# The order of large and small products in a column slot of a split-precision kernel

## The chip, the core and the metric

The kernel runs on one core of one Trainium2 chip. The metric is the device time of one execution in microseconds; the program's only output is a 256 x 1024 array of float32. Before the change the median of three timed runs is 1666.28 us (1665.99 to 1666.77).

## The reference

Two transformer blocks run on the same 256 tokens, of width 1024. The first has two layers: FFN, a mixer (attention beside a gated linear recurrence in the first layer, a gated short convolution in the second), FFN. The second has one: FFN, a mixer (a Fourier part beside a bidirectional state-space scan), FFN; another 256 tokens of context go through its first FFN and a part of its mixer. Between them these make seven passes through an FFN of this form, with norms and residuals around it:

```
def swiglu(h, w_gate, w_up, w_down):
    return (jax.nn.silu(h @ w_gate) * (h @ w_up)) @ w_down
```

The shapes are 256 x 1024 for `h`, 1024 x 2816 for `w_gate` and `w_up`, 2816 x 1024 for `w_down`. The short convolution's mixer begins with a product of `h` with a matrix of 1024 x 3072. All of this is float32.

## The kernel before, in words

Every float32 operand of a large product is split into two parts of lower precision, `hi` and `lo`, and a product is made of three: hi x hi, lo x hi, hi x lo. ACT writes the `hi` part of a weight tile (`w_hi`, line 1135), DVE the `lo` part (`w_lo`, line 1768), from tiles of 128 x 1024 that SP's queue brings in. Such a tile is a slot; the stream has 564, and eight lie in a ring that both parts share. TensorE (PE) does the products in the order in which the code issues them; no scheduler moves them.

An FFN runs in eleven steps of 256 of its 2816 columns, each with four slots for gate and up and two for the product with `w_down` (`down_slot`, line 539, 512-column products into the bank `dn`). In the first FFN all steps have the activations as the stationary operand (`wide_slot`, line 494). In the other six, steps 2 to 9 do it the other way round: a slot holds 128 columns of the weight for all eight k-tiles, and the weights are the stationary operand. These are the column slots (`column_slot`, lines 515 to 529), four in a row into the four banks `gu[0]`, `gu[1]`, `tp[0]`, `tp[1]`, so six FFNs with eight steps make 48 groups of four. Behind each group stand the two `down_slot`s of the step before. In front of it stand, as a rule, the two of the step before that; in eight groups a transposition lies between (lines 635 and 659). The short convolution's mixer, `sc`, has 24 more column slots (lines 871 and 874).

A column slot makes its three products with two instructions for a k-tile:

- the large one, 512 columns: `w_hi` stationary, and `hT[:, :, k, :]` moving, which is `hi` and `lo` of the activations side by side (lines 524 and 528), into the whole bank `o`
- the small one, 256 columns: `w_lo` stationary, `hi` of the activations moving (lines 525 and 527), added to the first half of the bank

The two halves of the bank are added later by another engine. Each product has a weight load ahead of it, of 128 x 128, which the profile shows as PEld. Before a slot's first product TensorE waits for the slot's `w_lo` (`lo_ready`), and the last one signals `slot_used`.

Of the kernel before, what the change touches and what calls it, by code (L numbers as in the profile page):

```python
# [23 lines left out]
KT = D // P  # L24
TOK = 256
# [112 lines left out]
def build(nc, weights, ada_w, x_in, ctx_in, pre_rows, post_rows, small, mod, out):  # L138
    with ExitStack() as stack:
        def sb(name, shape, dt=F32):  # L140
            return stack.enter_context(nc.sbuf_tensor(name, shape, dt))
# [5 lines left out]
        w_hi = sb("w_hi", [P, RING, SLOT], F32R)  # L147
        w_lo = sb("w_lo", [P, RING, SLOT], F32R)
        hT = sb("hT", [P, 2, KT, TOK], F32R)
        hT_hi, hT_lo = hT[:, 0, :, :], hT[:, 1, :, :]  # L150
# [301 lines left out]
        def _(pe):  # L452
# [62 lines left out]
            def column_slot(n, o, at_half=lambda: None):  # L515

                pe.wait_ge(lo_ready, n + 1)
                r = n % RING
                for k in range(KT):
                    if k == KT // 2:  # L520
                        at_half()
                    c = slice(k * P, (k + 1) * P)
                    if k == 0:
                        pe.matmul(o, w_hi[:, r, c], hT[:, :, k, :], start=True, stop=False)  # L524
                        pe.matmul(o[:, 0:TOK], w_lo[:, r, c], hT_hi[:, k, :], start=False, stop=False)  # L525
                    else:
                        pe.matmul(o[:, 0:TOK], w_lo[:, r, c], hT_hi[:, k, :], start=False, stop=False)  # L527
                        m = pe.matmul(o, w_hi[:, r, c], hT[:, :, k, :], start=False, stop=k == KT - 1)  # L528
                m.then_inc(slot_used, 1)

            def down_slot(n, acts, k, start=False, stop=False, used=True):
# [95 lines left out]
            def ffn(s, n0):  # L627
# [50 lines left out]
                for j in range(2, STEPS - 1):  # L678
                    n = n0 + 10 + 6 * (j - 2)
                    if s == 0:  # L680
                        if j > 2:
                            act_transposed(j - 1)
                        for si in range(4):
                            wide_slot(n + si, si, both)
                        down(n + 4, j - 1)
                        continue
                    for si in range(4):
                        if j > 2 and si % 2 == 0:
                            pe.wait_ge((gate_summed, up_summed)[si // 2], COLUMN_N[s, j - 1])
                        elif si == 2:  # L690
                            pe.wait_ge(actT_lo_ready, TURN_N[s, 1, None])
                        if si == 3 and (s, j - 1) in ADA_TURN:
                            pe.wait_ge(mod_biased, 1 + ADA_TURN[s, j - 1])
                        column_slot(n + si, column_bank(si))
                    down(n + 4, j - 1)
                    if (s, j) in ADA_TURN:
                        pe.wait_ge(up_summed, COLUMN_N[s, j])
                        mod_transposed(ADA_TURN[s, j])
# [159 lines left out]
            def sc(s, n0):  # L858
                for q in range(3 * KT):
                    if q == 1:  # L860
                        context_x_tokens(1)
                    if q == 4:
                        context_b_tokens()
                    if q == 7:
                        context_states()
                    if q == 8:
                        pe.wait_ge(state_ready, 2)
                    if SC_BEFORE[q] is not None:
                        pe.wait_ge(sc_summed, SC_BEFORE[q] + 1)
                    if q:  # L870
                        column_slot(n0 + q, sc_bank(q))
                    else:
                        pe.wait_ge(hT_lo_ready, 2 * TT * s + TT)
                        column_slot(n0, sc_bank(0), lambda: pe.wait_ge(hT_lo_ready, 2 * TT * (s + 1)))
                out_proj(s, n0 + 3 * KT, range(KT), [[MIX0["sc"] + 1 + k // 2] * TT for k in range(KT)], apart=(0, 1))
# [1838 lines left out]
```

## Time and profile before

| | before |
|---|---|
| median of three timed runs | 1666.28 us |
| span of the profiled execution | 1665.4 us |
| PE busy | 1655.6 us (99%), 8756 products |
| PEld (weight loads) busy | 1415.4 us (85%) |
| DVE busy | 1229.5 us (74%) |
| ACT busy | 927.8 us (56%) |
| PE's share of the chain that ended last | 94% |
| lines 527 and 528 in `gu` and `tp`, share of the chain | 10% for each bank pair at 528, 5% at 527 |

The profiled execution's time is its span, 1665.4 us; the median of the timed runs lies 0.9 us above it. Products are pipelined: one lasts longer (0.39 us for 512 columns) than the time from its start to the next start. So PE's busy time says only that it is never idle. How long a row of products takes is read from the starts in the time line.

### The profile page before, as it was taken

Reading aid. Unit: us, or ns where it says so; the run is one execution under the profiler, and the core shown is the slowest. Engines: PE = TensorE matmul, PEld = TensorE weight load, DVE = VectorE, ACT = ScalarE, POOL = GpSimd, SP = SyncE. Lnnn points to the kernel's source line nnn. Section 1 sums busy time; section 2 is a strip of 40 time slices with the busy share of each in tenths; the row PEclk is TensorE's granted clock in tenths of the full one; section 3 lists DMA queues with packets and bytes.
Section 4 is the critical chain, followed back from the end, with each engine's and each line's share of the span. In section 5 each row is a group of like instructions: output and inputs, shape, how many; then the busy total and the mean of one; then the engine's idle time right before and its main releaser. Section 6 shows DMA issues by size and latency. Waiting matters only on the chain.

```text
span 1665.4 us, 22804 instructions
## 1 busy us (share of the span) xinstructions
PE 1655.6 (99%) x8756; PEld 1415.4 (85%) x8756; DVE 1229.5 (74%) x1630; ACT 927.8 (56%) x1396; POOL 148.0 (9%) x210
## 2 busy tenths in 40 slices
PE   9999999999999999999999999999999999999998
PEld 7888888888888888888899888888888889988887
DVE  6888776788888777776688876655766668986564
ACT  6655577655555455545566455554645458655553
POOL 1100100000211001110010011000002012310000
PEclk9999999999999999999999999999999999999999
DMA  8977552787859876687655557554667545357551
GB/s 292 340 261 258 170 191 103 248 295 256 286 174 334 261 247 215 258 301 256 203 166 182 169 174 265 200 189 141 225 213 252 186 144 203 108 180 244 189 190 64
DMA packets 99356, 359.32 MB, mean 216 GB/s; under 512 B 11184, under 2 KB 11440, under 8 KB 99248
## 3 DMA queue, kind: packets, MB, share of 16 engines
q1 hardware_dynamic: 92736, 335.59, 59.0%
q0 software_dynamic: 6368, 22.21, 4.3%
q8 instruction: 69, 1.13, 0.3%
q14 instruction: 39, 0.32, 0.1%
q10 hardware_dynamic: 144, 0.07, 0.0%
HBM read 356.70 MB, written 1.12 MB: 215 GB/s over the span
## 4 chain that ended last, share of the span: by engine, by line
PE 94%; DVE 3%; DMA 2%; issue 1%; ACT 0%; SPq 0%; DVEq 0%; POOLq 0%; POOL 0%; ACTq 0%
PE dn L539 28%; PE gu L494 19%; PE gu L528 10%; PE tp L528 10%; PE gu L527 5%; PE tp L527 5%; PE dn L509 4%; DMA raw<-in_weights 2%; PE gu L524 1%; PE tp L524 1%; PE tp L457 1%; PE dn L528 1%; PE gu L525 1%; PE tp L525 1%; PE dn L494 1%; DVE w_lo L1768 1%
## 5 line engine op out<-in xcount | busy, mean ns | idle before, releaser
L1768 DVE TENSOR_TENSOR w_lo<-raw,w_hi 128x1024 fp32r<-128x1024 f32 x520 | 639.2, 1240 | 217.3 <-ACT w_hi L1135 212.4
L1135 ACT ACTIVATE w_hi<-raw 128x1024 fp32r<-128x1024 f32 x520 | 549.4, 1059 | 322.5 <-PE dn L539 147.7
L494 PE MATMUL gu<-w_hi,hT 128*128 128x512 f32 x1056 | 328.9, 393 | 1.6 <-DVE w_lo L1764 1.1
L528 PE MATMUL gu<-hT,w_hi 128*128 128x512 f32 x728 | 259.6, 396 | 0.0
L528 PE MATMUL tp<-hT,w_hi 128*128 128x512 f32 x728 | 259.5, 396 | 0.0
L539 PE MATMUL dn<-w_hi,actT_hi 128*128 128x512 f32 x608 | 238.8, 393 | 0.0
L539 PE MATMUL dn<-w_lo,actT_hi 128*128 128x512 f32 x608 | 236.9, 390 | 0.0
L539 PE MATMUL dn<-w_hi,actT_lo 128*128 128x512 f32 x608 | 236.7, 389 | 0.0
L494 PEld LDWEIGHTS gu<-w_hi,hT 128*128 128x128 f32 x1056 | 195.6, 188 | 42.6 <-DVE hT L1776 1.5
L494 PE MATMUL gu<-w_lo,hT 128*128 128x512 f32 x528 | 205.9, 390 | 0.0
L527 PE MATMUL gu<-hT,w_lo 128*128 128x256 f32 x728 | 203.1, 279 | 0.0
L527 PE MATMUL tp<-hT,w_lo 128*128 128x256 f32 x728 | 203.0, 279 | 0.0
L528 PEld LDWEIGHTS gu<-hT,w_hi 128*128 128x128 f32 x728 | 136.6, 188 | 28.2
L528 PEld LDWEIGHTS tp<-hT,w_hi 128*128 128x128 f32 x728 | 136.6, 188 | 28.2
L527 PEld LDWEIGHTS tp<-hT,w_lo 128*128 128x128 f32 x728 | 137.3, 189 | 4.8
L527 PEld LDWEIGHTS gu<-hT,w_lo 128*128 128x128 f32 x728 | 137.2, 189 | 4.5
L1912 DVE CUSTOM_DVE_ANT_0 arena<-arena 128x1024 f32<-128x1024 f32 x112 | 135.8, 1239 | 0.3
L539 PEld LDWEIGHTS dn<-w_lo,actT_hi 128*128 128x128 f32 x608 | 114.1, 188 | 24.2
L539 PEld LDWEIGHTS dn<-w_hi,actT_lo 128*128 128x128 f32 x608 | 114.2, 188 | 23.4
L539 PEld LDWEIGHTS dn<-w_hi,actT_hi 128*128 128x128 f32 x608 | 114.2, 188 | 21.2
L494 PEld LDWEIGHTS gu<-w_lo,hT 128*128 128x128 f32 x528 | 99.1, 188 | 21.0
L2467 POOL TENSOR_SCALAR ms<-ssq 128x1 f32<-128x1 f32 x42 | 16.8, 400 | 933.0 <-ACT junk L1166 919.3
(366 smaller groups left out, 2092.3 us busy)
## 6 DMA issues: line engine op xcount, KB each, us to landing
raw<-in_weights SPq DMA_DIRECT2D x563, 512.0 KB, 4.3
arena<-in_ada_w SPq DMA_DIRECT2D x72, 512.0 KB, 4.3
post_row<-in_post_rows POOLq DMA_DIRECT2D x10, 512.0 KB, 5.6
pre_row<-in_pre_rows POOLq DMA_DIRECT2D x10, 512.0 KB, 7.2
mod_row<-mod POOLq DMA_DIRECT2D x9, 512.0 KB, 10.0
shift_row<-mod POOLq DMA_DIRECT2D x5, 512.0 KB, 9.8
x<-in_x_in SPq DMA_DIRECT2D x4, 256.0 KB, 6.0
arena<-in_c_rows POOLq DMA_DIRECT2D x2, 512.0 KB, 9.3
```

What stands on the lines that cost most here:

```text
L457: m = pe.transpose(in_bank(s, t, half)[:, q * P:(q + 1) * P], rows[:, t, k * P:(k + 1) * P], ident[:])
L494: m = pe.matmul(bank, h[:, k, t * P:(t + 1) * P], w[:, r, kk * 512:(kk + 1) * 512], start=k == 0 and q == 0, stop=k == KT - 1 and q == 2)
L509: m = pe.matmul(o, w[:, r, k * P:(k + 1) * P], h[:, k, :], start=k == 0 and q == 0, stop=k == KT - 1 and q == 2)
L524: pe.matmul(o, w_hi[:, r, c], hT[:, :, k, :], start=True, stop=False)
L525: pe.matmul(o[:, 0:TOK], w_lo[:, r, c], hT_hi[:, k, :], start=False, stop=False)
L527: pe.matmul(o[:, 0:TOK], w_lo[:, r, c], hT_hi[:, k, :], start=False, stop=False)
L528: m = pe.matmul(o, w_hi[:, r, c], hT[:, :, k, :], start=False, stop=k == KT - 1)
L539: m = pe.matmul(dn[:, t, c], a[:, k, :], w[:, r, c], start=start and q == 0, stop=stop and q == 2)
L1135: act.activation(o, i, ACT.Copy, **kw).then_inc(done, 1)
L1768: dve.tensor_tensor(w_lo[:, r, :], raw[:, n % RAW, :], w_hi[:, r, :].bitcast(F32), ALU.subtract).then_inc(lo_ready, 1)
L1912: m = dve.tensor_tensor_reduce(ada_out[:, v, :], w, c_row[:, v, :], 1.0, 0.0, ALU.mult, ALU.add, mod_cols[:, i, v:v + 1])
L2467: pool.tensor_scalar(ms[:, c], ssq[:, c, 0], eps, None, ALU.add).then_inc(pool_step, 1)
```

## The change

In a column slot the first k-tile had its large product first and the other seven their small product first. Now every k-tile has the large product first and the small one behind it. The first large product opens the bank's sum as before; the last small product closes it and signals `slot_used`, where it was the last large one. The products, their operands and their number stay the same. In the short convolution's first slot the wait in the middle (`at_half`) stands ahead of a large product now, where it was a small one.

```
-                    if k == 0:
-                        pe.matmul(o, w_hi[:, r, c], hT[:, :, k, :], start=True, stop=False)
-                        pe.matmul(o[:, 0:TOK], w_lo[:, r, c], hT_hi[:, k, :], start=False, stop=False)
-                    else:
-                        pe.matmul(o[:, 0:TOK], w_lo[:, r, c], hT_hi[:, k, :], start=False, stop=False)
-                        m = pe.matmul(o, w_hi[:, r, c], hT[:, :, k, :], start=False, stop=k == KT - 1)
+                    pe.matmul(o, w_hi[:, r, c], hT[:, :, k, :], start=k == 0, stop=False)
+                    m = pe.matmul(o[:, 0:TOK], w_lo[:, r, c], hT_hi[:, k, :], start=False, stop=k == KT - 1)
```

PE at the start of a group behind a row of 512-column products (line 539, the second column group of the second FFN), before the change:

```order
L539 MATMUL dn<-w_lo,actT_hi 128x512
L524 MATMUL gu<-hT,w_hi 128x512
L525 MATMUL gu<-hT,w_lo 128x256
L527 MATMUL gu<-hT,w_lo 128x256
L528 MATMUL gu<-hT,w_hi 128x512
L527 MATMUL gu<-hT,w_lo 128x256
L528 MATMUL gu<-hT,w_hi 128x512
```

The same place now, where line 523 is the large product, line 524 the small one, and line 535 is what was 539:

```order
L535 MATMUL dn<-w_lo,actT_hi 128x512
L523 MATMUL gu<-hT,w_hi 128x512
L524 MATMUL gu<-hT,w_lo 128x256
L523 MATMUL gu<-hT,w_hi 128x512
L524 MATMUL gu<-hT,w_lo 128x256
L523 MATMUL gu<-hT,w_hi 128x512
L524 MATMUL gu<-hT,w_lo 128x256
```

The third product of the group was a small one and is a large one; the second small one moved one place back.

PE at the border between the first and the second slot of that group, before the change:

```order
L527 MATMUL gu<-hT,w_lo 128x256
L528 MATMUL gu<-hT,w_hi 128x512
L524 MATMUL gu<-hT,w_hi 128x512
L525 MATMUL gu<-hT,w_lo 128x256
L527 MATMUL gu<-hT,w_lo 128x256
L528 MATMUL gu<-hT,w_hi 128x512
```

The same border now:

```order
L523 MATMUL gu<-hT,w_hi 128x512
L524 MATMUL gu<-hT,w_lo 128x256
L523 MATMUL gu<-hT,w_hi 128x512
L524 MATMUL gu<-hT,w_lo 128x256
L523 MATMUL gu<-hT,w_hi 128x512
L524 MATMUL gu<-hT,w_lo 128x256
```

The two large products in a row at the border and the two small ones behind them are gone.

## Rows read from the trace of the kernel before

**Rows 1.** The page: PE's busy time, the granted clock, the chain by engine.

```profile
PE 1655.6 (99%) x8756; PEld 1415.4 (85%) x8756; DVE 1229.5 (74%) x1630; ACT 927.8 (56%) x1396; POOL 148.0 (9%) x210
...
PEclk9999999999999999999999999999999999999999
...
PE 94%; DVE 3%; DMA 2%; issue 1%; ACT 0%; SPq 0%; DVEq 0%; POOLq 0%; POOL 0%; ACTq 0%
```

**Rows 2.** PE's waits: line, engine waited for, us in total, times, longest.

```profile
PE dn L594 <- DVE actT_hi L2441: 1.5, 1, 1.5
```

**Rows 3.** Time line of PE, one group: start us, us, engine, line, operation.

```profile
340.73 0.39 PE L524 MATMUL gu<-hT,w_hi 128*128 128x512 f32 x1
340.95 0.28 PE L525 MATMUL gu<-hT,w_lo 128*128 128x256 f32 x1
341.07 0.28 PE L527 MATMUL gu<-hT,w_lo 128*128 128x256 f32 x1
341.19 0.40 PE L528 MATMUL gu<-hT,w_hi 128*128 128x512 f32 x1
...
343.19 0.28 PE L527 MATMUL gu<-hT,w_lo 128*128 128x256 f32 x1
343.31 0.40 PE L528 MATMUL gu<-hT,w_hi 128*128 128x512 f32 x1
343.54 0.40 PE L524 MATMUL gu<-hT,w_hi 128*128 128x512 f32 x1
...
344.00 0.40 PE L528 MATMUL gu<-hT,w_hi 128*128 128x512 f32 x1
...
346.08 0.40 PE L528 MATMUL gu<-hT,w_hi 128*128 128x512 f32 x1
346.32 0.39 PE L524 MATMUL tp<-hT,w_hi 128*128 128x512 f32 x1
...
349.13 0.40 PE L524 MATMUL tp<-hT,w_hi 128*128 128x512 f32 x1
...
351.91 0.39 PE L539 MATMUL dn<-w_hi,actT_hi 128*128 128x512 f32 x1
```

**Rows 4.** Line 524, whole program: counts, durations ns min/median/max, first and last start.

```profile
L524 PE MATMUL gu<-hT,w_hi x104: 389/397/501, 324.0 to 1623.4; 128*128 128x512 f32 x104
...
L524 PE MATMUL tp<-hT,w_hi x104: 393/397/527, 329.7 to 1629.0; 128*128 128x512 f32 x104
...
L524 PE MATMUL dn<-hT,w_hi x8: 389/395/398, 917.0 to 947.8; 128*128 128x512 f32 x8
```

**Rows 5.** Lines 528 and 527 from 341.2 to 343.3 us.

```profile
L528 PE MATMUL gu<-hT,w_hi x6: 395/398/403, 341.2 to 343.0; 128*128 128x512 f32 x6
...
L527 PE MATMUL gu<-hT,w_lo x7: 278/281/284, 341.1 to 343.2; 128*128 128x256 f32 x7
L527 PEld LDWEIGHTS gu<-hT,w_lo x6: 188/190/192, 341.2 to 343.0; 128*128 128x128 f32 x6
```

**Rows 6.** Lines 528 and 527 from 344.02 to 346.07 us.

```profile
L528 PE MATMUL gu<-hT,w_hi x6: 392/394/395, 344.0 to 345.7; 128*128 128x512 f32 x6
...
L527 PE MATMUL gu<-hT,w_lo x7: 274/274/280, 343.9 to 346.0; 128*128 128x256 f32 x7
L527 PEld LDWEIGHTS gu<-hT,w_lo x6: 187/188/188, 344.0 to 345.7; 128*128 128x128 f32 x6
```

**Rows 7.** Line 525 at 341.0 us.

```profile
L525 PE MATMUL gu<-hT,w_lo x1: 278/278/278, 341.0 to 341.0; 128*128 128x256 f32 x1
```

**Rows 8.** Line 525's weight load behind a transposition, at 324.1 us.

```profile
L525 PEld LDWEIGHTS gu<-hT,w_lo x1: 192/192/192, 324.1 to 324.1; 128*128 128x128 f32 x1
```

**Rows 9.** Time line of PE, first and last start of 16 convolution slots.

```profile
916.98 0.39 PE L524 MATMUL dn<-hT,w_hi 128*128 128x512 f32 x1
...
961.72 0.39 PE L539 MATMUL dn<-w_hi,actT_hi 128*128 128x512 f32 x1
```

**Rows 10.** The chain of waits from 860 to 915 us: start us, us, what.

```profile
869.65 7.68 DMA raw<-in_weights
```

## The prediction

> **What bounds the kernel now.** I read the page first, then TensorE's waits, the time line of one group of column slots, and last the durations inside single slots. The engine table has PE busy in 1655.6 of 1665.4 us, the clock row is at its top in every slice (2.4 GHz, the higher of its two levels), and the chain that ended last lies on PE for 94% [rows 1]. The waits agree: the longest total that PE spends on another engine is 1.5 us [rows 2]. So TensorE is the bound, what counts is the distance from the start of one product to the start of the next, and a nanosecond that the change adds there is a nanosecond of the whole, as long as no other engine is then late. None becomes late when TensorE gets slower.
>
> The reader is to look at starts, not at busy times. A large product (512 columns) starts 0.23 us before the next, a small one (256) about 0.12 us before it. Inside a column slot they already alternate. In the slot at 340.73, from the large product at 341.19 to the one at 343.31, there are six pairs in 2.12 us: 0.3533 us a pair. In the next slot, from 344.00 to 346.08, six like pairs take 2.08 us: 0.3467 [rows 3]. The instructions are the same, at the same clock, and nothing waits between them. So there are two paces, which I call loose and tight, and a slot keeps the one that it has to its end. The four slots take 2.81, 2.78, 2.81 and 2.78 us: the pace changes at every slot border [rows 3]. That border is where the alternation breaks: two large products in a row (343.31, 343.54), then two small ones. The change takes away just these breaks.
>
> **The change part by part.** It removes no product, adds none and moves no wait to another engine: 216 slots (104 + 104 + 8) [rows 4] of eight large and eight small products each. In a slot the order "large, small, small, large, small, large ..." becomes "large, small, large, small ...", also across the border to the next slot. What is moved is the order alone, so the sum has one big term: which pace an unbroken group runs at.
>
> By columns the swap is free: two large products in a row start 0.23 apart (343.31, 343.54) and two small ones 0.12 (340.95, 341.07), so two of each cost what two pairs cost [rows 3]. By paces it is not. Without a break nothing flips the pace, so all four slots of a group run at the one with which it begins. Groups of four (eight in each of six FFNs, 48 by the loops) follow a row of 512-column products in 40 cases. There the first slot is at the loose pace, behind one large and two small ones. In the new order the first three starts are the same up to 341.07, since what starts there, at 0.34 us behind the first large one, hangs on what lies before it. It is a large product now, not a small one.
>
> Is the state at that point that of the loose or of the tight pace? The durations of the records tell them apart. Small products last 278, 281 or 284 ns at the loose pace [rows 5] and 274 or 280 at the tight [rows 6]; the first small one of the group lasts 278 [rows 7]. That value occurs in the loose cycle alone, where a large product follows it, as it will now. So I take it that the group enters the loose cycle and stays in it.
>
> The sum, in the times of the profiled execution: the first pair 0.34 (340.73 to 341.07), 31 pairs at 0.3533 make 10.95, together 11.29 us, against 11.18 (340.73 to 351.91) [rows 3]. That is 0.11 us a group, and 48 groups make 5.4 us. The eight groups that follow a transposition, not a 512-column product, I count alike: the load before their first small product lasts 192 ns [rows 8], a length that the loads of the loose slot reach and those of the tight slot (188 at most) do not [rows 5, 6]. If they run tight instead, each gives about 0.09 back rather than costing 0.11, and the sum is 8 x 0.2 = 1.6 us lower.
>
> The 24 column slots of the short convolution: 16 of them in a row take 44.74 us (916.98 to 961.72), 2.796 each [rows 9]. At the loose pace a slot is 8 x 0.3533 = 2.827, so 0.031 more, 0.7 us for 24. Seven of these lie before 914 us, where the chain goes by way of a weight transfer of 7.68 us [rows 10]; if that hides their share, 0.2 is lost from the sum.
>
> The end of a group: its last product is a small one now, and 512-column products follow. No row shows this change of step at the loose pace. Six pairs at the two paces differ by 0.04 us, and I bound one change of step by half of that, 0.02 either way for each group, 1 us in all, and count nothing. The signal that a slot is done now hangs on the small product. A large one at 343.31 lasts 0.40 and ends 0.17 behind the start of the next (343.54); a small one of 0.28 that starts 0.12 before the next (343.19, 343.31) ends 0.16 behind it. No reader of the banks is later.
>
> Sum: 5.4 + 0.7 = 6.1 us, so a span of about 1671.5. The median of the timed runs (1666.28) lies 0.9 above the profiled span, which gives 1672.4.
>
> **The rivals.** *Tight throughout.* If the third instruction of a group falls into the tight cycle, 32 pairs at 0.3467 take 11.09 us, 0.09 less than now, 4.3 us for 48 groups; the short convolution gives 24 x (2.796 - 2.773) = 0.5. The time is then 1661.5, on the other side. For it: the tight pace is in the trace in every second slot, and once in it, nothing breaks it now. Against it: none of the 40 groups behind a 512-column row starts with it. The point that decides is the first large product behind the first small one.
>
> *The flip has another cause.* Each slot's first product also carries the wait for its weights. If that flips the pace and not the order, loose (2.827) and tight (2.773) slots go on taking turns, 11.20 a group, 0.02 more than now: about 1 us, 1667.3. Against it: two starts at the border lie 0.23 apart (343.31, 343.54), as between any large product and its next.
>
> *Order does not matter.* Then it is 1666.3. The rows speak against it with 2.12 and 2.08 us for the same six pairs. [...]
>
> **How the numbers follow.** Loose throughout 0.80, tight throughout 0.09, flip at the wait 0.06, no effect of order 0.05. About 0.2% (3.3 us) is what a measurement of this kernel can tell from no change, so the first is slower, the second faster, and the last two are the same. The forecast's own range is 1672.4 less 1.6, 0.2 and 1.0, so 1669.6, to 1673.4 with the 1.0 on top; widened a little above for what surrounds the span, 1674. To hold 8 in 10 with room, it reaches down to the flip at the wait, 1667.2. Tight throughout and no effect of order, 0.14 in all, lie outside.
>
> **What would show it.** In the changed profile the starts of the first large products of four slots would lie 2.83 us apart and a group would take 11.29 us, the large products of every slot would last 395 to 403 ns, as in [rows 5], and none 392, as in [rows 6]. Slots of 2.77 and a largest duration of 395 would show the tight pace. Slots of 2.83 and 2.77 in turn would show that the wait flips it. If the groups come out at 11.29 and the time does not rise by 5 us or more, something outside the column slots gave it back, and the step that calls TensorE the bound is wrong.

## The result and the profile after

The changed kernel is slower by 0.4%: 1673.62 us median of five runs (1673.28 to 1675.38) against 1666.77 (1665.99 to 1667.19), a ratio of 1.0041 (95% interval 1.0030 to 1.0052). The forecast was 1672.4. The 1666.28 from which it started was the median of the first three of the five runs before.

The page and the waits of the changed kernel, to be read against [rows 1, 2]. Line numbers behind the change are four lower (539 is 535 now); line 523 is the large product and line 524 the small one.

```profile
PE 1663.2 (99%) x8756; PEld 1417.6 (85%) x8756; DVE 1230.2 (74%) x1630; ACT 927.5 (55%) x1396; POOL 150.8 (9%) x210
...
PEclk9999999999999999999999999999999999999999
...
PE 95%; DVE 2%; DMA 2%; issue 0%; ACT 0%; SPq 0%; DVEq 0%; POOLq 0%; POOL 0%; ACTq 0%
```

```profile
PE dn L590 <- DVE actT_hi L2437: 1.5, 1, 1.5
```

TensorE does the same 8756 products at the same clock, and its longest wait is again 1.5 us: it is as busy as before and needs longer. The time line of the group that answers to [rows 3] says where. The columns are start, duration, engine, line, operation.

```profile
342.19 0.39 PE L523 MATMUL gu<-hT,w_hi 128*128 128x512 f32 x1
...
342.53 0.40 PE L523 MATMUL gu<-hT,w_hi 128*128 128x512 f32 x1
...
342.88 0.40 PE L523 MATMUL gu<-hT,w_hi 128*128 128x512 f32 x1
...
343.24 0.40 PE L523 MATMUL gu<-hT,w_hi 128*128 128x512 f32 x1
...
343.59 0.40 PE L523 MATMUL gu<-hT,w_hi 128*128 128x512 f32 x1
...
345.00 0.40 PE L523 MATMUL gu<-hT,w_hi 128*128 128x512 f32 x1
...
347.83 0.40 PE L523 MATMUL tp<-hT,w_hi 128*128 128x512 f32 x1
...
350.66 0.40 PE L523 MATMUL tp<-hT,w_hi 128*128 128x512 f32 x1
...
353.48 0.40 PE L535 MATMUL dn<-w_hi,actT_hi 128*128 128x512 f32 x1
353.72 0.40 PE L535 MATMUL dn<-w_hi,actT_lo 128*128 128x512 f32 x1
353.96 0.40 PE L535 MATMUL dn<-w_lo,actT_hi 128*128 128x512 f32 x1
...
358.99 0.39 PE L523 MATMUL gu<-hT,w_hi 128*128 128x512 f32 x1
```

The four slots take 2.81, 2.83, 2.83 and 2.82 us, the group 11.29; before, 2.81 and 2.78 took turns and made 11.18. Behind the first pair the pairs take 0.35, 0.36 and 0.35 us (342.53 to 343.59), 1.06 for three, and these three lengths repeat to the end of the group. The second thing to see is behind the group: the 24 products of 512 columns take 5.51 us (353.48 to 358.99), and the first of them start 0.24 apart. Before, the same 24 took 5.44, from 351.91 in [rows 3] to this start in the kernel before:

```profile
357.35 0.39 PE L524 MATMUL gu<-hT,w_hi 128*128 128x512 f32 x1
```

Large products in the second slot of that group, to be compared with [rows 5] (loose) and [rows 6] (tight); the numbers are min/median/max in ns:

```profile
L523 PE MATMUL gu<-hT,w_hi x8: 395/398/403, 345.0 to 347.5; 128*128 128x512 f32 x8
```

These are the durations of a loose slot, where the second slot was a tight one. Not all is loose. Here are the short convolution's slots that answer to [rows 9], and large products there:

```profile
921.39 0.39 PE L523 MATMUL dn<-hT,w_hi 128*128 128x512 f32 x1
...
965.77 0.39 PE L535 MATMUL dn<-w_hi,actT_hi 128*128 128x512 f32 x1
```

```profile
L523 PE MATMUL dn<-hT,w_hi x48: 392/394/395, 926.9 to 954.3; 128*128 128x512 f32 x48
```

Sixteen slots take 44.38 us, 2.774 each, where they took 2.796: tight from end to end. Of the eight slots of the convolution ahead of this row four are loose: the first, which stands alone, and three that stand together behind a transposition (line 904). The second of these three takes 2.83:

```profile
907.77 0.40 PE L523 MATMUL gu<-hT,w_hi 128*128 128x512 f32 x1
...
910.60 0.40 PE L523 MATMUL tp<-hT,w_hi 128*128 128x512 f32 x1
```

The groups of four behind the short transposition (line 655) are tight. The slots of one of the two:

```profile
409.37 0.27 PE L655 MATMUL tp<-first,mod_cols 128*48 128x128 f32 x1
409.39 0.48 PE L523 MATMUL gu<-hT,w_hi 128*128 128x512 f32 x1
...
412.25 0.39 PE L523 MATMUL gu<-hT,w_hi 128*128 128x512 f32 x1
...
415.02 0.39 PE L523 MATMUL tp<-hT,w_hi 128*128 128x512 f32 x1
...
417.80 0.39 PE L523 MATMUL tp<-hT,w_hi 128*128 128x512 f32 x1
...
420.57 0.39 PE L535 MATMUL dn<-w_hi,actT_hi 128*128 128x512 f32 x1
```

Behind the first slot, which overlaps with the transposition, the starts lie 2.77 and 2.78 apart. Added up from the starts in both traces, in us:

| | before | after | difference |
|---|---|---|---|
| 40 groups behind 512-column products | 447.30 | 451.60 | +4.30 |
| the 24 products behind each of them | 217.77 | 220.14 | +2.37 |
| 6 groups behind the long transposition, and the products behind | 100.45 | 101.13 | +0.68 |
| 2 groups behind the short one, and the products behind | 33.47 | 33.32 | -0.15 |
| 24 convolution slots | 67.58 | 67.18 | -0.40 |
| sum | | | +6.80 |

The medians differ by 6.85. The profiled spans differ by more, 1673.6 less 1665.4, because that one execution took 1675.38 us, 1.8 above the median; the first group in it starts at 325.3 us instead of 324.0 [rows 4], and the change touches nothing ahead of that.

### The profile page after: what moved, and what is told of

The parts are those of the page before. It is cut to its first block, busy times and chain, and to the rows that moved or that the text cites. A ratio compares the mean times of both kernels' runs of the same rounds, so it can differ in the third digit from the quotient of the medians.

```text
span 1673.6 us, 22804 instructions
## 1 busy us (share of the span) xinstructions
PE 1663.2 (99%) x8756; PEld 1417.6 (85%) x8756; DVE 1230.2 (74%) x1630; ACT 927.5 (55%) x1396; POOL 150.8 (9%) x210
## 4 chain that ended last, share of the span: by engine, by line
PE 95%; DVE 2%; DMA 2%; issue 0%; ACT 0%; SPq 0%; DVEq 0%; POOLq 0%; POOL 0%; ACTq 0%
PE dn L535 28%; PE gu L494 19%; PE gu L523 12%; PE tp L523 12%; PE tp L524 6%; PE gu L524 6%; PE dn L509 5%; DMA raw<-in_weights 2%; PE tp L457 1%; PE dn L523 1%; DVE w_lo L1760 1%; PE gu L509 1%; PE dn L494 1%; PE dn L524 0%; DMA x<-in_x_in 0%
## 5 line engine op out<-in xcount | busy, mean ns | idle before, releaser
L523 PE MATMUL gu<-hT,w_hi 128*128 128x512 f32 x832 | 296.4, 399 | 0.0
L523 PE MATMUL tp<-hT,w_hi 128*128 128x512 f32 x832 | 295.8, 398 | 0.0
L524 PE MATMUL tp<-hT,w_lo 128*128 128x256 f32 x832 | 233.5, 281 | 0.0
L524 PE MATMUL gu<-hT,w_lo 128*128 128x256 f32 x832 | 233.4, 281 | 0.0
L523 PEld LDWEIGHTS tp<-hT,w_hi 128*128 128x128 f32 x832 | 156.3, 188 | 38.6
L523 PEld LDWEIGHTS gu<-hT,w_hi 128*128 128x128 f32 x832 | 156.3, 188 | 38.0 <-DVE hT L1772 0.3
L524 PEld LDWEIGHTS gu<-hT,w_lo 128*128 128x128 f32 x832 | 157.1, 189 | 1.6
L524 PEld LDWEIGHTS tp<-hT,w_lo 128*128 128x128 f32 x832 | 157.1, 189 | 0.0
```

The costliest lines, as they stand in the source:

```text
L523: pe.matmul(o, w_hi[:, r, c], hT[:, :, k, :], start=k == 0, stop=False)
L524: m = pe.matmul(o[:, 0:TOK], w_lo[:, r, c], hT_hi[:, k, :], start=False, stop=k == KT - 1)
```

## The experiments

**Same sizes together.** All eight large products of a slot first, then all eight small ones.

```
-                    c = slice(k * P, (k + 1) * P)
-                    pe.matmul(o, w_hi[:, r, c], hT[:, :, k, :], start=k == 0, stop=False)
-                    m = pe.matmul(o[:, 0:TOK], w_lo[:, r, c], hT_hi[:, k, :], start=False, stop=k == KT - 1)
+                    pe.matmul(o, w_hi[:, r, k * P:(k + 1) * P], hT[:, :, k, :], start=k == 0, stop=False)
+                for k in range(KT):
+                    m = pe.matmul(o[:, 0:TOK], w_lo[:, r, k * P:(k + 1) * P], hT_hi[:, k, :], start=False, stop=k == KT - 1)
```

> Every column slot does its eight large products first and then its eight small ones, so that the size changes twice in a slot and not sixteen times; the small product is still the last one. Theory (the loss is in the alternation, at the loose pace of 353 ns a pair): products of one size in a row start 227 ns apart (512 columns) and 120 ns apart (256 columns, as the attention mixer's column products show in the kernel before), so a slot takes 8 x 0.227 + 8 x 0.120 = 2.77 us and a group 11.09 to 11.14, in every one of the 48 groups; the time is 1661.5 to 1664.5 us, below the kernel before (1666.8) and some 10 us below the changed one. Rival 1 (the cost hangs on the small product standing last in the slot, with the signal): 11.29 us a group and 1673 us, as in the changed kernel. Rival 2 (order does not matter to the whole; something outside the slots made the 7 us): 1673 us with groups of 11.1.

Measured: 1667.15 us, ratio to the kernel before 1.0001 (0.9992 to 1.0010). A group in its time line (equal products in a row are one line, x8; the last line is where the next group starts):

```profile
341.89 1.98 PE L522 MATMUL gu<-hT,w_hi 128*128 128x512 f32 x8
...
344.66 2.00 PE L522 MATMUL gu<-hT,w_hi 128*128 128x512 f32 x8
...
347.45 2.00 PE L522 MATMUL tp<-hT,w_hi 128*128 128x512 f32 x8
...
353.04 0.40 PE L535 MATMUL dn<-w_hi,actT_hi 128*128 128x512 f32 x1
...
358.51 0.39 PE L522 MATMUL gu<-hT,w_hi 128*128 128x512 f32 x1
```

The group takes 11.15 us and the products behind it 5.47, 16.62 together as in the kernel before. Rivals 1 and 2 fall: the small product still stands last, and 6.5 us of the 7 are gone. But my size was wrong too: 1661.5 to 1664.5 us were expected. The first slot takes the 2.77 us of the sum of its products; each later one takes 2.79, and the products behind a group 0.02 more than in the kernel before. So a run of small products followed by large ones costs some 0.02 us, and sorting by size is no cure.

**Orders.** One order for each step of an FFN (H is a large product, l a small one), all in one kernel; the lines between are left out:

```
+ALT, OLD = "Hl" * 8, "Hll" + "Hl" * 6 + "H"
+B8, B4, B2, ABBA = "H" * 8 + "l" * 8, ("H" * 4 + "l" * 4) * 2, "HHll" * 4, "HllH" * 4
+def broken(p):
+    return "Hl" * p + "HHll" + "Hl" * (6 - p)
...
-                        column_slot(n + si, column_bank(si))
+                        column_slot(n + si, column_bank(si), order=ORDERS[FFNS.index(s) % 2][j][si])
```

> A probe with another order in each step of an FFN, read group by group from the starts. Theory (a pace that alternation keeps and that only a break of the alternation can change; loose behind a row of 512-column products): four slots strictly alternating 11.29 us; four in the old order 11.18; blocks of eight 11.09 to 11.14, blocks of four the same, pairs (two large, two small) 11.1 to 11.2; large-small-small-large repeated about 11.1 to 11.2. One old slot and then three alternating ones tells whether two large products in a row are enough to change the pace: 2.81 + 3 x 2.77 = 11.13 if so, 2.81 + 3 x 2.83 = 11.30 if not. Three alternating slots and an old one has two small ones in a row alone. Two large and two small ones in a row once in the second slot: the rest of the group at 2.77 a slot, about 11.17, if any such break changes the pace; 11.29 if it hangs on the point of the cycle at which the break comes. Rival (no pace that lasts; each change of size costs its own time): the time of a group grows with the number of changes, the same in all slots, alternating slots 2.83 wherever they stand, also behind an old one.

Measured, behind 512-column products (slots, group, and the 24 products behind it, in us; each value came out alike in every FFN that has it, within 0.003):

| order | slots | group | behind |
|---|---|---|---|
| four alternating | 2.810, 2.830, 2.831, 2.819 | 11.290 | 5.503 |
| four old | 2.813, 2.777, 2.817, 2.777 | 11.182 | 5.444 |
| three alternating, one old | 2.810, 2.830, 2.831, 2.821 | 11.292 | 5.461 |
| one old, three alternating | 2.813, 2.814, 2.831, 2.820 | 11.277 | 5.503 |
| two old, two alternating | 2.813, 2.777, 2.814, 2.830 | 11.233 | 5.467 |
| blocks of eight | 2.766, 2.793, 2.794, 2.793 | 11.146 | 5.467 |
| one slot in blocks of eight, three alternating | 2.766, 2.832, 2.819, 2.830 | 11.247 | 5.467 |
| blocks of four | 2.780, 2.806, 2.807, 2.807 | 11.200 | 5.486 |
| two large, two small | 2.777, 2.787, 2.786, 2.787 | 11.137 | 5.450 |
| large, small, small, large | 2.783, 2.786, 2.787, 2.787 | 11.143 | 5.444 |
| one break behind 9 pairs | 2.810, 2.828, 2.819, 2.830 | 11.287 | 5.467 |
| one break behind 10 pairs | 2.810, 2.794, 2.773, 2.773 | 11.150 | 5.450 |
| one break behind 11 pairs | 2.810, 2.817, 2.773, 2.774 | 11.174 | 5.467 |

The row with the break behind 10 pairs in the time line; the last slot is at 2.77:

```profile
424.35 0.39 PE L540 MATMUL gu<-hT,w_hi 128*128 128x512 f32 x1
...
432.73 0.40 PE L540 MATMUL tp<-hT,w_hi 128*128 128x512 f32 x1
...
435.50 0.40 PE L553 MATMUL dn<-w_hi,actT_hi 128*128 128x512 f32 x1
```

The rival falls: alternating slots take 2.773 or 2.830 us by what stands before them, and blocks of four, with fewer changes of size than pairs, take longer (11.200 us; 11.09 to 11.14 were expected). A first slot in blocks of eight leaves the alternating slots behind it loose. Two large products alone, without the two small ones, do not bring a loose group to the tight pace at the border where both kinds together do (one old, three alternating), and they throw a tight one out of it (two old, two alternating). One break of both kinds brings the tight pace at two points of three.

**Where the break stands.** Breaks in the first slot, and more repeated orders (the second list goes on):

```
+ORDERS = [{2: [broken(1)] + [ALT] * 3, **{3 + p: [broken(p)] + [ALT] * 3 for p in range(7)}},
+          {2: [PAIRS] * 4, 3: [ABBA] + [ALT] * 3, 4: [PAIRS] + [ALT] * 3, ...
```

> A second probe, again with an order for each step: in half of the FFNs one break (two large products, then two small ones) in the first slot of a group, behind 0 to 6 pairs, and strict alternation after it; in the other half, repeated orders (pairs; threes; large products one or two ahead of the small ones). In the probe before, a break behind 10 pairs left the rest of the group at 2.77 us a slot, one behind 11 pairs did so after a loss, and one behind 9 left it at 2.83. Theory (the loose pace is a cycle of three pairs, and a break changes the pace when it falls on one point of that cycle): breaks behind 1 and 4 pairs (10 less 9 and less 6) lead to 2.77 us in the three slots that follow and a group of 11.10 to 11.13; behind 2 and 5 the same with some loss (11.15 to 11.18); behind 0, 3 and 6 the slots that follow take 2.82 to 2.83, and the group 11.27 to 11.29. Rival 1 (any break changes the pace, and the one behind 9 failed by chance): 2.77 behind all seven. Rival 2 (what decides is the distance from the slot's border or its wait, not the cycle): the three breaks in the second slot stood 1, 2 and 3 pairs behind its border, so 2, 3 change the pace here too and 1 does not. The price of the 512-column products behind a group: 5.45 to 5.47 where it ends tight, 5.50 where it ends loose on a small product.

Measured: breaks behind 0, 1, 2, 3, 4, 5 and 6 pairs give groups of 11.287, 11.093, 11.110, 11.287, 11.110, 11.134 and 11.287 us. The break behind 1 pair, and the one behind 3:

```profile
1046.75 0.39 PE L539 MATMUL gu<-hT,w_hi 128*128 128x512 f32 x1
...
1049.52 0.39 PE L539 MATMUL gu<-hT,w_hi 128*128 128x512 f32 x1
...
1057.84 0.39 PE L552 MATMUL dn<-w_hi,actT_hi 128*128 128x512 f32 x1
...
1079.87 0.39 PE L539 MATMUL gu<-hT,w_hi 128*128 128x512 f32 x1
...
1091.15 0.40 PE L552 MATMUL dn<-w_hi,actT_hi 128*128 128x512 f32 x1
...
1096.62 0.39 PE L539 MATMUL gu<-hT,w_hi 128*128 128x512 f32 x1
```

The same 64 products take 11.09 or 11.29 us (11.28 by these rounded starts); the two orders differ only in the place at which one small product and the large one behind it have changed places. The period of three is as forecast, with a somewhat smaller loss behind 2 and 5. Both rivals fall: not any break does it, and the distance from the border of a slot would have let 3 succeed and 1 fail.

The products behind a tight group take 5.45 or 5.47 us. My price for the loose ones was wrong: behind 0, 3 and 6 pairs the group ends loose on a small product, and 5.47 follow (1091.15 to 1096.62), not 5.50. The groups of the changed kernel that are followed by 5.50 have a last slot of 2.82; the loose ones here, and five of the six behind the changed kernel's long transposition, have a last slot of 2.83 and are followed by 5.47. So the point of the cycle at which a group ends goes with the price behind it.

The best of the other half is one slot in pairs and then three alternating: 11.097 and 5.450. Blocks of four in the first slot also lead to the tight pace (11.105, but 5.482 behind); large, small, small, large in it leads to the loose one (11.258).

**Width of the small product.**

```
+WIDTHS = {2: 256, 3: 256, 4: 272, 5: 288, 6: 320, 7: 384, 8: 224, 9: 192}
...
-                    m = pe.matmul(o[:, 0:TOK], w_lo[:, r, c], hT_hi[:, k, :], start=False, stop=k == KT - 1)
+                    m = pe.matmul(o[:, 0:width], w_lo[:, r, c], hT_row[:, k * TOK:k * TOK + width], start=False, stop=k == KT - 1)
```

> The changed kernel with the small product's columns varied by the FFN's step: 256, 256, 272, 288, 320, 384, 224 and 192 in steps 2 to 9 (the first half's sum takes in other activations where it is wider, and leaves some out where it is narrower, so the output is not the reference's). Own pace of a pair: (512 + w) / 2.4 + 2 x 13.3 ns, from 227 ns for products of 512 columns in a row: 347, 353, 360, 373, 400, 333, 320 ns for 256, 272, 288, 320, 384, 224, 192. Theory 1 (the small product is just as long as the weight load that has to lie behind it, and the loose pace is that load coming late): the loss over the own pace is 6 to 7 ns a pair at 256, and nothing from 272 or 288 columns on; with 224 and 192 a pair stays near 347 to 353, a loss of 15 to 30 ns. Theory 2 (each change of size costs, whatever the sizes): a loss of 6 to 7 ns a pair at every width.

Measured: the later slots of a group take 2.880, 2.907, 3.040, 3.253, 2.747 and 2.720 us at 272, 288, 320, 384, 224 and 192 columns. Divided by eight that is 360.0, 363.3, 380.0, 406.7, 343.4 and 340.0 ns a pair, so 6.7, 3.3, 6.7, 6.7, 10 and 20 ns above the own pace, which is the estimate of the expectation; no row of one size was measured at these widths. Two slot starts at 384 columns:

```profile
601.33 0.40 PE L527 MATMUL gu<-hT,w_hi 128*128 128x512 f32 x1
...
604.58 0.40 PE L527 MATMUL tp<-hT,w_hi 128*128 128x512 f32 x1
```

Theory 1 falls in its main part: a small product with half as many columns again leaves the loss where it was. Below 256 columns a pair gets little shorter, which would fit a load that sets the pace there; that is not shown. Theory 2 has the right size at four widths, but at 288 it is half, and at 256 the tight pace has no loss at all. Nor has a width one loss: behind the short transposition the later slots take 3.306 us at 384 columns and 2.750 to 2.760 at 192, so the entry counts there too. What inside TensorE loses these nanoseconds stays open.

**The changed kernel with its pace set.** From this follows a version: the first slot of a group in pairs, the others alternating; all four in pairs behind the long transposition.

```
-                        column_slot(n + si, column_bank(si))
+                        column_slot(n + si, column_bank(si), order=PAIRS if j == 2 or si == 0 and (s, j - 1) not in ADA_TURN else ALT)
```

> The changed kernel with another order in the first slot of a group alone: two large and two small products four times over, then three strictly alternating slots; behind the long transpositions (step 2) all four slots in pairs, behind the short one all four alternating, and the short convolution alternating. Theory (the pace is set by how a group is entered): 11.10 us for each of the 40 groups behind 512-column products, with 5.45 for the 24 products behind them, 0.08 less than the kernel before for both together (11.18 + 5.44), 3.1 us in all; the other eight groups 0.04 to 0.07 less each, 0.4; the convolution 0.4. Together 3.9 us below the kernel before: ratio 0.9976, some 11 us below the changed kernel, from which only the order in one slot of four is different. Rival (the changed kernel is slower because of the alternation itself or because a slot ends with its small product): 28 of 32 slots of an FFN... are such slots here too in three of four cases, so at most a quarter of the 7 us goes away: 1671 to 1673 us.

Measured: 1663.11 us, ratio to the kernel before 0.9976 (0.9965 to 0.9987). It is faster than both kernels, than the one before by 0.24%.

```profile
340.42 0.62 PE L530 MATMUL gu<-hT,w_hi 128*128 128x512 f32 x2
...
351.52 0.40 PE L543 MATMUL dn<-w_hi,actT_hi 128*128 128x512 f32 x1
...
356.97 0.39 PE L530 MATMUL gu<-hT,w_hi 128*128 128x512 f32 x1
```

11.10 and 5.45 us, as expected. In the 40 groups behind 512-column products three slots of four are the changed kernel's own, word for word (only the six groups behind the long transposition differ in all four), and some 10 us are between the two times. The rival, with 1671 to 1673 us, falls.

**The changed kernel again.**

> The changed kernel once more, on the same chip as the run beside it: 1673 to 1674 us, groups of 11.29 us behind 512-column products, 5.50 us for the products behind them, and 2.77 us a slot in the short convolution.

Measured beside the run above: 1673.66 us, ratio 1.0037 (1.0024 to 1.0050), with the same groups behind 512-column products:

```profile
341.10 0.39 PE L523 MATMUL gu<-hT,w_hi 128*128 128x512 f32 x1
...
352.39 0.40 PE L535 MATMUL dn<-w_hi,actT_hi 128*128 128x512 f32 x1
...
357.89 0.39 PE L523 MATMUL gu<-hT,w_hi 128*128 128x512 f32 x1
```

In the short convolution 2.77 us a slot came out for most slots, but again not for three that stand together. They are three others, one transposition earlier, where the first execution was tight; those that were loose in it are tight here. The second slot of either three:

```profile
897.97 0.40 PE L523 MATMUL tp<-hT,w_hi 128*128 128x512 f32 x1
...
900.79 0.40 PE L523 MATMUL tp<-hT,w_hi 128*128 128x512 f32 x1
...
907.27 0.39 PE L523 MATMUL gu<-hT,w_hi 128*128 128x512 f32 x1
...
910.05 0.39 PE L523 MATMUL tp<-hT,w_hi 128*128 128x512 f32 x1
```

They take 2.82 us and 2.78 us, by the same instructions in the same order. So behind a transposition the order alone does not decide the pace; what else differed between the two executions is not known.

## Why the prediction was right, and where it was not

**What bounds the kernel.** Right: the lengths of the column slots and of what follows them add up to 6.80 of 6.85 us.

**The pace of an unbroken group.** Right, and the main term with it: 40 groups at 0.11 us were forecast, 4.30 us in all were measured. But the mark by which the entry was read, the first small product's 278 ns, does not tell the paces apart: in the kernel before it lasts 277 at the head of the tight slot as well.

```profile
L525 PE MATMUL gu<-hT,w_lo x1: 277/277/277, 343.8 to 343.8; 128*128 128x256 f32 x1
```

So it was in part luck that the entry was called right. The probes bear out the step behind it, that a group keeps the pace with which it is entered: with one break at the right place the same slots run at 2.77 us.

**What flips the pace at a border.** Half right. I put it down to the two large products and the two small ones together, and at the border where the old order has them the two large ones alone are not enough; the two small ones alone were tried at one place (three alternating, one old), where the slot stays at 2.821 us. But a break also has to come at the right point of the loose cycle, which the old order's slot length happened to meet. Nothing in the argument showed that.

**The eight groups behind a transposition.** Forecast as loose, 0.9 us. The six behind the long one are loose; the two behind the short one are tight. With the products behind them, 0.53 was measured. Their mark, a load of 192 ns, was read at a long one and stands at a short one too:

```profile
L525 PEld LDWEIGHTS gu<-hT,w_lo x1: 192/192/192, 407.3 to 407.3; 128*128 128x128 f32 x1
```

And in the kernel before the slot behind that long transposition ran at the tight pace, six pairs in 2.08 us, in spite of the mark:

```profile
324.54 0.40 PE L528 MATMUL gu<-hT,w_hi 128*128 128x512 f32 x1
...
326.62 0.40 PE L528 MATMUL gu<-hT,w_hi 128*128 128x512 f32 x1
```

**The convolution.** Wrong in sign: +0.7 forecast, -0.40 measured. The step that failed took the loose pace over to slots that are not entered from 512-column products, without a row for it. Four of the 24 slots are loose even so, and for three of them which they are changed from one execution to the other.

**The end of a group.** The largest miss: "I bound it by 0.02 either way for each group, 1 us in all, and count nothing". It is 0.06 us for each of the 40, 2.37 in all. What the group leaves behind does not stop with its last small product: products of equal size behind it still start up to 0.24 us apart before they settle at 0.227. It is not a price of the loose pace as such. With an old slot as the last of a loose group the 24 products fall to 5.461 us, though the group itself is as long (11.292), and behind the loose groups that end at another point of the cycle they take 5.47. That the total came out near the forecast is luck: the 2.37 that this term missed were largely made up by some 1.7 us that the other terms had too much, 1.1 of them in the convolution.

**The rivals.** *Tight throughout* is what most of the convolution and two groups do, and what the version with its pace set reaches in the 40 groups; it needs the right entry. *The flip at the wait* falls: every border still has its wait, and the pace stays. *Order does not matter* falls on the same 64 products in 11.09 or 11.29 us.

## What to carry to other kernels

When TensorE is the bound and never idle, read the distance between starts over several repeats of the loop and not one mean: two lengths for the same instructions show that there is something to win. An order that looks smoother can hold the worse of two paces; try what stands at the entry of a run of products, since it can decide about all of it, and look at more than one execution. A cost that a change leaves behind its own instructions has to be looked for in the next ones.

## What the runs showed of the hardware

Strictly alternating products of 512 and 256 columns, each with its own weight load, run at 347 or 353 ns a pair at the same clock, and stay there: 16 slots (128 pairs) in a row at the tight one. The loose pace repeats every three pairs (0.35, 0.35 and 0.36 us), and the point at which a break comes decides by that period: behind 0, 3, 6 or 9 pairs the group stays loose, behind 1, 2, 4, 5, 10 or 11 it becomes tight. Runs of one size start 227 ns (512 columns) apart; blocks of eight lose some 20 ns a slot, blocks of four 33 and pairs 13, against the 2.773 us of a tight slot. Which part of TensorE holds this state between products is not known from these runs.
